# Projecting v of two attention groups with the tokens on the partitions

## What is computed

```python
SEQ, D_MODEL, ATT_HEADS, ATT_HEAD_DIM = 1024, 1024, 8, 64
ATT_GROUPS = ((128, 1), (512, 4), (2048, 16))      # window, dilation
...
h = rmsnorm(x, norm_w)
z = h @ w_in
...
q_b = apply_rope(aqkv[:, :, 0], cos, sin)
k_b = apply_rope(aqkv[:, :, 1], cos, sin)
v_b = aqkv[:, :, 2]                                 # no rope on v
for g, (window, dilation) in enumerate(ATT_GROUPS):
    o_g, m_g, l_g = dilated_window_attention(q_b[:, :, g], k_b[:, :, g], v_b[:, :, g], window, dilation)
...
num = jnp.sum(wts[..., None] * jnp.stack(outs), axis=0)
o_b = (num / den[..., None]).reshape(B, S, ATT_DIM) * jax.nn.silu(ag)
```

## Time and profile before

| | |
|---|---|
| time, median of 3 runs | 1440.6 us (1439.61 to 1441.48) |
| profiled execution, its own time | 1440.21 us |
| its span, first to last instruction | 1438.4 us |
| TensorE matmul busy | 1417.5 us, 99% |
| TensorE weight load busy | 1202.4 us, 84% |
| VectorE busy | 958.1 us, 67% |
| ScalarE busy | 660.0 us, 46% |
| GpSimd busy | 34.8 us, 2% |
| mean granted TensorE clock | 1.000 |

### The profile page before, as it was taken

One profiled execution on the slowest core, in us unless ns is written; L12 is line 12 of the kernel. 1 busy time (PEld: TensorE's weight loads), 2 busy tenths in 40 slices (PEclk: granted clock), 3 DMA queues, 4 the chain that ended last, 5 costly groups with the idle time before them and its releaser, 6 DMA issues. The chain is left out here.

```text
span 1438.4 us, 21609 instructions
## 1 busy us (share of the span) xinstructions
PE 1417.5 (99%) x7508; PEld 1202.4 (84%) x7508; DVE 958.1 (67%) x1635; ACT 660.0 (46%) x977; POOL 34.8 (2%) x40
## 2 busy tenths in 40 slices
PE   7999999999999999999999999999999999999998
PEld 5888888888888888888888888888888889888987
DVE  7987868687868686878834784478546866544423
ACT  5455555565555555546333443344344356212211
POOL 0200000000000000013100000000000000000000
PEclk9999999999999999999999999999999999999999
DMA  5211212112121212334222223222222233333602
GB/s 213 90 55 49 74 59 74 58 61 71 58 73 58 73 57 75 107 113 115 62 76 59 60 59 91 71 51 63 83 59 61 58 119 116 135 121 114 249 30 88
DMA packets 37495, 120.65 MB, mean 84 GB/s; under 512 B 6248, under 2 KB 6568, under 8 KB 37416
## 3 DMA queue, kind: packets, MB, share of 16 engines
q1 hardware_dynamic: 37424, 119.67, 25.8%
HBM read 84.85 MB, written 22.12 MB: 74 GB/s over the span
## 5 line engine op out<-in xcount | busy, mean ns | idle before, releaser
L833 PE MATMUL z_ps<-h_hi,w_hi 128*128 128x512 f32 x704 | 278.5, 396 | 0.5 <-ACT zz L1587 0.5
L835 PE MATMUL z_ps<-h_hi,w_lo 128*128 128x512 f32 x704 | 274.6, 390 | 0.0
L834 PE MATMUL z_ps<-h_lo,w_hi 128*128 128x512 f32 x704 | 274.4, 390 | 0.0
L835 PEld LDWEIGHTS z_ps<-h_hi,w_lo 128*128 128x128 f32 x704 | 132.2, 188 | 28.2
L833 PEld LDWEIGHTS z_ps<-h_hi,w_hi 128*128 128x128 f32 x704 | 132.4, 188 | 26.6 <-issue 1.0
L834 PEld LDWEIGHTS z_ps<-h_lo,w_hi 128*128 128x128 f32 x704 | 132.3, 188 | 25.1
L1754 DVE TENSOR_TENSOR w_lo<-w_stage,w_hi 128x1024 fp32r<-128x1024 f32 x45 | 55.5, 1232 | 73.8 <-ACT w_hi L1257 73.6
L1527 ACT ACTIVATE pt<-pb 128x512 f32<-128x512 f32 (+1 forms) x80 | 43.4, 543 | 119.5 <-PE pb L1068 119.2
L1835 DVE TENSOR_TENSOR w_lo<-mix,w_hi 128x512 fp32r<-128x512 f32 x84 | 56.1, 689 | 54.7 <-ACT w_hi L1335 53.9
L871 PE MATMUL z_ps<-h_hi,w_hi 128*128 128x512 f32 x224 | 91.5, 408 | 0.0
L873 PE MATMUL z_ps<-h_hi,w_lo 128*128 128x512 f32 x224 | 87.9, 392 | 0.0
(11 more groups left out here) (335 smaller groups left out, 3271.0 us busy)
## 6 DMA issues: line engine op xcount, KB each, us to landing
w_stage<-w_in SPq DMA_DIRECT2D x44, 512.0 KB, 3.6
raw<-w_in SPq DMA_DIRECT2D x44, 512.0 KB, 3.4
z_swap<-zz SPq DMA_DIRECT2D x96, 128.0 KB, 2.3
gate_d<-gate SPq DMA_DIRECT2D x15, 512.0 KB, 3.1
x_in<-x SPq DMA_DIRECT2D x8, 512.0 KB, 7.4
o_a_d<-o_a SPq DMA_DIRECT2D x8, 512.0 KB, 2.7
w_stage<-w_a SPq DMA_DIRECT2D x8, 512.0 KB, 3.8
cos_t<-gate_d SPq DMA_DIRECT2D x8, 512.0 KB, 4.5
```

The lines of the kernel that those rows point to most:

```text
L833: nc.tensor.matmul(z_ps[hf][:], w_hi[s][:, k, :], h_hi[:, k, t], start=k == 0, stop=False)
L834: nc.tensor.matmul(z_ps[hf][:], w_hi[s][:, k, :], h_lo[:, k, t], start=False, stop=False)
L835: last = nc.tensor.matmul(z_ps[hf][:], w_lo[s][:, k, :], h_hi[:, k, t], start=False, stop=k == KT - 1)
```

## The change

v of group 0 and 1 is projected by a new function `project_v`. There the roles are swapped: a block of 128 tokens of h is stationary, and the 128 columns of the weights move. The result has tokens on the partitions at once, and ScalarE writes it from `z_ps` straight into `vb`. Group 1 takes its tokens in residue order by reading every fourth one as the stationary operand. A half is four blocks; each needs 8 k x 3 matmuls of 128 columns, 96 in all. Group 2 keeps the old way with its eight transposes in slot 18. The counts of `avt_made` and `av_taken` shrink to one and two a pair, and the first score of a pair also waits until both banks `z_ps` of the previous pair are taken. In the first pair `project_v` is called once for both parts of a slot.

```diff
@@ SP @@
-                    sp.wait_ge(avt_made, 3 * PAIRS)
+                    sp.wait_ge(avt_made, PAIRS)
@@ TensorE, scores_t @@
-                    pe.wait_ge(av_taken, i * 6)
+                    pe.wait_ge(av_taken, i * 2)
+                    for s in range(2):
+                        pe.wait_ge(z_taken[s], N_HG + i * AT_CHUNKS)
@@ TensorE @@
+            def project_v(n, s, hf, g):
+
+                r = DILATIONS[g]
+                for blk in range(4 * hf, 4 * hf + 4):
+                    per = NB // r
+                    tokens = lambda t, k: t[:, k, :].rearrange("p (i r) -> p r i", r=r)[:, blk // per, P * (blk % per):P * (blk % per + 1)]
+                    dst = z_ps[hf][:, P * (blk % 4):P * (blk % 4 + 1)]
+                    for k in range(KT):
+                        if k == 0 and blk % 4 == 0:
+                            if hf == 0:
+                                pe.wait_ge(w_lo_done, w_seq(n))
+                            pe.wait_ge(z_taken[hf], n)
+                        nc.tensor.matmul(dst, tokens(h_hi, k), w_hi[s][:, k, :], start=k == 0, stop=False)
+                        nc.tensor.matmul(dst, tokens(h_hi, k), w_lo[s][:, k, :], start=False, stop=False)
+                        last = nc.tensor.matmul(dst, tokens(h_lo, k), w_hi[s][:, k, :], start=False, stop=k == KT - 1)
+                last.then_inc(z_made[hf], 1)
@@ TensorE, attention @@
-                            project(N_HG + c, c % 2, slot % 2, range(4 * part_of, 4 * part_of + 4))
+                            if c in (6, 7):
+                                if part_of == 0:
+                                    project_v(N_HG + c, c % 2, slot % 2, c - 6)
+                            else:
+                                project(N_HG + c, c % 2, slot % 2, range(4 * part_of, 4 * part_of + 4))
...
+                    elif cur and c in (6, 7):
+                        project_v(N_HG + i * AT_CHUNKS + c, c % 2, slot % 2, c - 6)
...
-                    if cur and slot in (14, 16, 18):
-                        g = (slot - 14) // 2
+                    if cur and slot == 18:
                         for s in range(2):
-                            pe.wait_ge(z_taken[s], N_HG + i * AT_CHUNKS + 7 + g)
-                        if g:
-                            pe.wait_ge(av_taken, i * 6 + 2 * g)
+                            pe.wait_ge(z_taken[s], N_HG + i * AT_CHUNKS + 9)
@@ ScalarE, attention @@
-                    if cur and slot in (15, 17, 19):
-                        g = (slot - 15) // 2
-                        act.wait_ge(avt_made, i * 3 + g + 1)
+                    if cur and slot == 19:
+                        act.wait_ge(avt_made, i + 1)
...
-                                act.wait_ge(avt_made, i * 3)
+                                act.wait_ge(avt_made, i)
...
-                            if g == 0 and hf == 0:
-                                act.wait_ge(rope_sum, i * 6 + 5)
-                            elif hf == 0:
-                                act.wait_ge(avt_made, i * 3 + g)
-                            r = DILATIONS[g]
-                            w = HALF // r
-                            dst = v_t[:].rearrange("p (r i) -> p r i", r=r)[:, :, w * hf:w * (hf + 1)]
-                            nc.scalar.activation(dst, z_ps[hf][:].rearrange("p (i r) -> p r i", r=r), ACT.Copy).then_inc(z_taken[hf], 1)
+                            if g < 2:
+                                dst = vb[:, g, 4 * hf:4 * hf + 4, :].rearrange("p c (x e) -> p c x e", e=EDIM)[:, :, 0:3:2, :]
+                                src = z_ps[hf][:].rearrange("p (c x e) -> p c x e", c=4, x=2)
+                            else:
+                                if hf == 0:
+                                    act.wait_ge(rope_sum, i * 6 + 5)
+                                dst = v_t[:].rearrange("p (r i) -> p r i", r=DILATIONS[g])[:, :, HALF // DILATIONS[g] * hf:HALF // DILATIONS[g] * (hf + 1)]
+                                src = z_ps[hf][:].rearrange("p (i r) -> p r i", r=DILATIONS[g])
+                            nc.scalar.activation(dst, src, ACT.Copy).then_inc(z_taken[hf], 1)
```

More of the change, by code:

```diff
@@ L1568, in attention @@
                             nc.scalar.activation(q_hi2[h][rows, :], q_sh[2][h][rows, :], ACT.Copy).then_inc(q2_rounded, 1)
-                    if cur and slot in (15, 17, 19):
-                        g = (slot - 15) // 2
-                        act.wait_ge(avt_made, i * 3 + g + 1)
+                    if cur and slot == 19:
+                        act.wait_ge(avt_made, i + 1)
                         for b in range(2):
-                            dst = vb[:, g, 4 * b:4 * b + 4, :].rearrange("p c (x e) -> p c x e", e=EDIM)[:, :, 0:3:2, :]
+                            dst = vb[:, 2, 4 * b:4 * b + 4, :].rearrange("p c (x e) -> p c x e", e=EDIM)[:, :, 0:3:2, :]
                             nc.scalar.activation(dst, pb[:, b, :].rearrange("p (c x e) -> p c x e", c=4, x=2), ACT.Copy).then_inc(av_taken, 1)
```

## The result

The changed kernel takes 1618.2 us (median of 5 runs, 1618.0 to 1619.4) against 1440.7 us before: a ratio of 1.1234, 95% interval 1.1218 to 1.1249. The direction was as forecast, the size was not: 1513 was predicted, and the range ended at 1600.

The account below looks back on a forecast made before the run. TensorE was taken as the bound. New projection 169.0 less old 87.3 gives +81.7; less 7.0 for transposes and 2 for waits, +72.7 on 1440.6 makes 1513 us. The range was 1505 to 1600.

Parts of the forecast that it names:

- The bound: In the attention stage TensorE sets the end; its added instructions cost their step, and relieving VectorE or ScalarE gives nothing.
- The step of a contiguous pair: In the new projection, each load with its 128-column matmul takes 0.110 us, set by the load; 1536 make 169.0 us.
- The removed projection, the transposes, the waits: Time taken off TensorE: 384 projection matmuls 87.3 us, transposes of groups 0 and 1 7.0 us, waits at maxima 2 us.
- The new wait behind the last pair: The first score waits until both banks of the ag chunk are taken, holding TensorE only behind the last pair; cost 0.
- Reading h as the stationary operand: Group 1's loads of every fourth token cost no more than contiguous ones: 0 taken, bounds 0 and +84 us.
- Rival A: Strided loads of h for group 1 are slow: 768 x 0.11 = +84 us, total 1597 us; chance 0.27.
- Rival D: The clock falls to the 1.2 GHz level in the new halves, doubling the step: +169, about 1682 us; chance 0.02.
- Main case: In the new projection all loads, strided ones too, step by 0.110 us: 1513 us in total; chance 0.62.
- B: In the new projection the second load of the same h_hi block is dropped or free: total 1462 us; chance 0.05.
- C: In the new projection another buffer hides every load, the step is 59 ns: total 1434 us; chance 0.04.
- the 81 ns a pair: The Trainium skill's figure for a sustained load and 128-column matmul: new projection 124 us, total 1468 us; not adopted.

Follow-up runs that it names:

- group-0 kernel: The kernel before with the change for v of group 0 alone; group 1 keeps its transposes and copies: 1478.5 us, 1.026 times before.
- contiguous kernel: The changed kernel, but group 1 reads its 128 stationary tokens side by side, without the residue order: 1515.9 us, 1.052 times before.
- the four executions with the 4.9 us wait: Change for group 0 alone, with half of k of group 2 and half of v of group 0 issued in turn: three 1603 to 1605 us, one 1575.7.

## Why the prediction was right or wrong

*The bound.* Right: TensorE sets the end, its share is still 99%, VectorE's unchanged 958 us cost nothing.

*The step of a contiguous pair.* Right: 0.110 predicted, 0.1115 measured, loads recorded with 192 ns where 188 was named. The short fp32r row L1068 with its load, and the start times of loads, were the rows that carried it. For 1536 pairs it makes 171.3 in place of 169.0 us.

*The removed projection, the transposes, the waits.* Right as a sum: the group-0 kernel and the contiguous one land within 1 us of sums made of 87.3, 7.0 and 2.4. In the contiguous kernel the waits at 837.54 and 849.85 have no counterpart.

*The new wait behind the last pair.* Right. In the contiguous kernel TensorE now waits for the gate's bank, and the first weighted sum starts 2.56 us behind the start of that eviction, as in the earlier trace rows (1182.60 - 1180.04):

```profile
1256.31 0.60 ACT L1288 ACTIVATE z_swap<-z_ps 128x512 f32<-128x512 f32 x1 [3.39 <-PE z_ps L835]
1256.93 1.28 ACT L1549 ACT_TABLE_LOAD   x1
...
1257.22 0.38 PE L1064 MATMUL pb<-mask_b,ident_b 128*128 128x512 bf16 x1 [0.94 <-issue]
...
1258.87 1.16 PE L1087 MATMUL pc<-pt,vb 128*128 128x128 f32 x8
```

*Reading h as the stationary operand.* This step failed, and with it the number. I took 0 from the copy of VectorE, 1.01 us for 1024 strided elements, "the only row with a single operand stream". That row tells how fast VectorE reads, not how fast TensorE's load does; its 0.99 ns per element is quicker than the 1.82 ns that the load needs per 16 bytes. Rival A was the truth, with a chance of 0.27. What the prediction quotes there, two hits in 16 bytes for full pace, pointed the right way, and the copy was no evidence against it for TensorE. Its price was low too: 0.11 us more per load was put for 0.122, 84 for 94 us (768 x 0.122). The upper end was one more load time, a guess at a factor of two; the true price has nothing to do with the load's own time.

*The clock.* Rival D named the array's idleness and doubled every step, for 0.02. What came was a mixture of A and D: the slow loads left the array with less to do (with 512 columns a load the clock stays at 1.00), the clock fell 3 us later, and that cost 9.3 us. In the halves themselves it cost nothing, since a strided load is no slower at 0.50. I had priced A and D as if each came alone.

*The range.* Main case 1513, with 2.3 for the step 1515; A adds 94, D's part 9: 1618. The range reached to A at its too low price (1597) and 3 us beyond, so a mispricing of 10 us and a follow-up of 9 both fell outside. An end that rests on a mechanism no row shows should have been wider by at least its own uncertainty.

*B and C* didn't come: every matmul has its load, and loads aren't free. Nor did the 81 ns a pair that the prediction weighed: it takes 0.1115 us here.

*What stays open:* why a stationary line costs twice a moving one, why the clock holds at 0.50 under short matmuls that hold it at 1.00, and why one of the four executions with the 4.9 us wait was 28 us quicker. What was not tried: a residue-sorted copy of h, which would make group 1 contiguous; by the contiguous kernel it would still end at 1516 us, an estimate without the price of the copy, above before. No version tried beats the kernel before.

## What to carry to other kernels

Count weight loads, not columns: with fp32r weights of 128 columns a matmul of 128 moving columns costs its load, here 0.111 us, and one of 256 hardly more (0.12), and only one load runs ahead, so long matmuls around it don't help. Swapping the operands turned 24 loads a half into 96: to save 0.9 us of transposes a chunk it spent 10.5 us more on the projection, even where the loads were contiguous. Keep what TensorE reads, the stationary side above all, at two or more fp32 per 16 bytes (the moving side was tried at one only). And price what a slow step does to the clock: a phase that is bound by loads can lose the 2.4 GHz level, or, once it is lost in a wait, not get it back.

## What the runs showed of the hardware that was not expected

- A load of 128 fp32r columns takes the longer of 0.111 us (0.213 at the granted clock of 0.50) and 1.82 ns for each 16-byte stretch per partition that it touches: 0.118 at step 2, 0.173 at step 3, 0.233 at step 4, 0.240 at step 8. The Trainium skill ("TensorE: Matmul & The Clock Gate", section on LDWEIGHTS) gives columns / 1.2 ns, an estimate of 107 ns for 128 columns; the traces agree to 5% at the high clock (0.111 us), and show 0.213 us at the low one.
- The moving side pays 0.90 ns for a token alone in its 16 bytes, 0.46 us for 512 at step 4.
- One load runs ahead of the running matmul: behind a 512-column matmul the second load starts only when that matmul's 0.227 us are over, and one long and four short ones take 0.675 us, the sum of their parts.
- The clock can hold at either level under the same contiguous short matmuls: at 1.00 over 45 us when they began at the high level, at 0.50 over 20 us when they began at the low one, and over some 52 us where long ones were mixed into the first half.
